# S5 inputs in three PSUM banks instead of two, the turned B and C blocks sharing one region beside y, and scans and y groups one ring step later

## The chip, the core and the metric

The kernel runs on one core of one Trainium2 chip. Its time is device microseconds of one execution, and the number compared is the median of several runs. TensorE (PE) does the matrix products, VectorE (DVE) and ScalarE (ACT) the elementwise work, GpSimd (POOL) some elementwise work on SBUF and the DMA issues of the tables, and SyncE (SP) issues the weight loads. All matmul results go to PSUM, eight banks of 512 float32 columns on each of 128 partitions.

## The reference, cut to what matters

Two transformer-like blocks run one after the other on a sequence of 256 tokens with 2048 features in float32. The change lies in the second one, in its S5 branch, a state space model of 64 groups with 64 complex states each:

```python
bu_re = jnp.einsum('bsgc,gpc->bsgp', uf, bb_re)      # inputs: 16 channels of a group into 64 states
bu_im = jnp.einsum('bsgc,gpc->bsgp', uf, bb_im)
...
_, _, xs_re, xs_im = lax.associative_scan(combine, (a_re, a_im, bu_re, bu_im), axis=1)
y = (jnp.einsum('bsgp,gcp->bsgc', xs_re, c_re.astype(f32))
     - jnp.einsum('bsgp,gcp->bsgc', xs_im, c_im.astype(f32)))
y = y.reshape(bsz, seq, D_SSM) + d_skip.astype(f32) * u.astype(f32)
y = jax.nn.gelu(y.astype(u.dtype))
return y * jax.nn.sigmoid(y @ w_glu + b_glu)
```

The dense products around it (`h @ w_in[l]` above all) fill most of the kernel's time.

## The kernel before, in words

**The ring.** Every dense product streams its weights through a ring of four slots. One ring step (a "subgroup") is two tiles of 128 rows by 512 columns of weights. SP loads it, ACT copies it to `w_hi` (line 658), DVE computes the rest `w_lo = raw - w_hi` (line 1148, `split_lo`), and PE multiplies (lines 1844 to 1847 where the output is by token in 256-column pieces of `h`, lines 1852 to 1854 with 512 columns; 12 matmuls of 512 columns or 24 of 256 a step). ACT and DVE work three steps ahead: in its step s each of them makes the slot of step s+3, and ACT may begin that only when PE is through with step s-1 (`pe_used`). A unit of work is eight steps, and at its end the accumulator is emptied.

**What stands beside the ring.** Other work is hung on ring steps: `places` is a list of (step, function), and in every engine's program the function stands behind that engine's own part of the step. Engines are strictly in order, so this list is the order of work. PE's function for step s stands behind the matmuls of step s, DVE's behind `w_lo` of step s+3. No planner changes it.

**S5.** There are 32 rotations n, each for two groups of states, and they begin at the steps `ROT_AT[n] = 1 + 17*n//8`: 1, 3, 5, 7, 9, 11, 13, 15, 18 and so on, eight rotations in 17 steps. Four rotations with the same n // 4 make a block c of 0 to 7. For one rotation:

- `bu_pair(n)`, for even n, PE at `ROT_AT[n] - 1`: eight small matmuls write the inputs of rotations n and n+1 into the PSUM banks `side[0]` and `side[1]`. It waits for `rot_ready` n, that is until DVE has read the inputs of all rotations up to n-1.
- `rotate_in(n)`, DVE at `ROT_AT[n]`: two multiplies of the bank with a table (lines 1630 and 1631) into one of two buffers, `tmp` or `k_t`.
- POOL adds and subtracts the two products (lines 575 and 576).
- `scan_out(n)`, DVE one step later: two scans (lines 1637 and 1639), and two multiplies into `prods[n % 4]` (line 1643). Behind it POOL issues the load of the table for rotation n+4 (line 567).

For one block c: `turn_b(c)` and `turn_c(c)` transpose the blocks of B and C into PSUM (`tps`), and ACT copies them out (`b_copy`, `c_copy`) three steps ahead of the block's first rotation and three steps behind it. `y_of(c)`, three steps behind the block's last rotation, adds up 16 matmuls into `tps[:, 512:768]`. `skip(c)` on DVE (line 1650), five steps behind the last rotation, reads y out of `tps`, and ACT's `gelu5(c)` follows. The tensor `tps` is two banks, columns 0 to 511 and 512 to 1023. Before the change, B and C lay in the first of them and y in the second.

Of the kernel before, what the change touches and what calls it, by code (L numbers as in the profile page):

```python
# [16 lines left out]
P = 128  # L17
# [4 lines left out]
ACT = mybir.ActivationFunctionType  # L22
# [72 lines left out]
def griffin_block_then_ssm_block(nc, a, inv_freq, out):  # L95
    with ExitStack() as ctx:
        def sb(name, shape, dt=F32):
            return ctx.enter_context(nc.sbuf_tensor(name, shape, dt))
# [7 lines left out]
        def ps(name, shape):  # L106
            return ctx.enter_context(nc.psum_tensor(name, shape, F32))
# [22 lines left out]
        ident = sb("ident", [P, P])  # L130
# [6 lines left out]
        v_tok = sb("v_tok", [P, TT, SEQ])  # L137
# [152 lines left out]
        u_feat, zs = slab_e[:, 0:8, :], slab_e[:, 8:16, :]  # L290
# [12 lines left out]
        c_t = mask[:, :].rearrange("p (n c) -> p n c", n=3)  # L303
        b_t = pi2[:, 0:4, :].rearrange("p a f -> p (a f)").rearrange("p (n c) -> p n c", n=2)
# [320 lines left out]
        ROT_AT = [1 + 17 * n // 8 for n in range(32)]  # L625
# [20 lines left out]
        def _(act):  # L646
# [34 lines left out]
            for rows, tile in ((FIRST_ROWS, 0), (SECOND_ROWS, 1)):  # L681
                at = 0
# [71 lines left out]
            for t in range(TT):  # L754
                ins = nc.scalar.activation(v_tok[:, t, :], tok(acc[0])[:, t, SEQ:2 * SEQ], ACT.Copy, scale=rstd[:, t:t + 1])
# [132 lines left out]
            for c in range(NH):  # L888
# [3 lines left out]
                for t in range(TT):  # L892
                    ins = nc.scalar.activation((tmp, tmp2)[c % 2][:, t, :], tok(acc[u % 2])[:, t, :], ACT.Square,
                                               accum_out=ssq[:, t, c:c + 1])
# [74 lines left out]
            for t in range(TT):  # L969
                act.wait_ge(e_final, t + 1)  # L970
                ins = nc.scalar.activation(tmp[:, t, :], e_tok[:, t, 3 * NC:], ACT.Square, accum_out=ssq[:, t, 3:4])
# [23 lines left out]

            def b_copy(c):
                act.wait_ge(b_turned, c + 1)
                nc.scalar.activation(b_t, tps[:, 0:2 * P].rearrange("p (n c) -> p n c", n=2), ACT.Copy).then_inc(b_copied, 1)

            def c_copy(c):  # L1000
                act.wait_ge(c_turned, c + 1)
                nc.scalar.activation(c_t[:, 0, :], tps[:, 2 * P:3 * P], ACT.Copy)
                nc.scalar.activation(c_t[:, 1:3, :], tps[:, 2 * P:4 * P].rearrange("p (n c) -> p n c", n=2), ACT.Copy,
                                     scale=-1.0).then_inc(c_copied, 1)

            def gelu5(c):
# [8 lines left out]
            places = [(S * (c + 1) + 3, lambda c=c: z_tanh_(c)) for c in range(2)]  # L1015
            for c in range(8):
                at = ROT_AT[4 * c]
# [6 lines left out]
            for c in range(8):  # L1024
# [19 lines left out]
            for c in range(2):  # L1044
# [53 lines left out]
            places = [(1, lambda: qk_copy(0))]  # L1098
# [7 lines left out]
            for i in range(NH):  # L1106
# [3 lines left out]
                for t in range(TT):  # L1110
                    ins = nc.scalar.activation(tmp[:, t, :], tok(acc[U_A % 2])[:, t, :], ACT.Tanh, scale=half_rstd[:, t:t + 1])
# [30 lines left out]
        def _(dve):  # L1142
# [159 lines left out]
            for t in range(TT):  # L1302
                both = stg[:, t, :].rearrange("p (h e u f) -> p h e u f", e=2, u=2, f=32)
                ins = rotate(tok(acc[0]), 4, t, [both[:, :, e] for e in range(2)], t == TT - 1)
# [194 lines left out]
            for c in range(NH):  # L1499
                u = U_OUT + c  # L1500
                at = slice(c * NC, (c + 1) * NC)
# [121 lines left out]
            def rotate_in(n):  # L1623


                t1, t2 = rot[n % 2]
                bu = side[n % 2][:, :].rearrange("p (n c) -> p n c", n=2)
                dve.wait_ge(table_landed[n % 4], 16 * (n // 4 + 1))
                dve.wait_ge(bu_ready, n // 2 + 1)
                V.tensor_tensor(t1, bu, tables[n % 4][:, 0:1, :].broadcast_to([P, 2, SEQ]), ALU.mult)  # L1630
                V.tensor_tensor(t2, bu, tables[n % 4][:, 1:2, :].broadcast_to([P, 2, SEQ]), ALU.mult).then_inc(rot_ready, 1)

            def scan_out(n):
                t1, t2 = rot[n % 2]
                decay = s5p[:, 3, n:n + 1].broadcast_to([P, SEQ])
                dve.wait_ge(mixed_ready, 2 * n + 1)
                chain.mark(V.tensor_tensor_scan(t1[:, 0, :], decay, t1[:, 0, :], 0.0, ALU.mult, ALU.add))  # L1637
                dve.wait_ge(mixed_ready, 2 * n + 2)
                chain.link(V.tensor_tensor_scan(t1[:, 1, :], decay, t1[:, 1, :], 0.0, ALU.mult, ALU.add))
                if n >= 4:  # L1640
                    dve.wait_ge(y5_ready, n // 4)
                for part in range(2):
                    ins = V.tensor_tensor(prods[n % 4][:, 2 * part:2 * part + 2, :], t1,
                                          tables[n % 4][:, part:part + 1, :].broadcast_to([P, 2, SEQ]), ALU.mult)
                ins.then_inc(out_ready, 1)
# [11 lines left out]
            places = [(S * (c - 1) + 1, lambda c=c: u_out(c)) for c in range(2)]  # L1657
            places += [(S * (c + 1) + 2, lambda c=c: z_out(c)) for c in range(2)]
            places += [(S * (c + 1) + 4, lambda c=c: z_silu(c)) for c in range(2)]
            for n in range(32):  # L1660
                places += [(ROT_AT[n], lambda n=n: rotate_in(n)), (ROT_AT[n] + 1, lambda n=n: scan_out(n))]
            for c in range(8):
                at = ROT_AT[4 * c + 3]
                places += [(at + 5, lambda c=c: skip(c)), (at + 7, lambda c=c: gelu_low(c))]
# [27 lines left out]
            for c in range(2):  # L1692
                steps(None, 0, G_GLU + c * 4, {1: [lambda: qk_mean_square(0)]} if c == 0 else {1: [lambda: qk_norm(0)]}, subgroups=4)
                at = slice(c * QPC, (c + 1) * QPC)
# [73 lines left out]
            places = []  # L1768
# [40 lines left out]
            for c in range(NH):  # L1809
# [3 lines left out]
                at = slice(c * NC, (c + 1) * NC)  # L1813
# [7 lines left out]
        def _(pe):  # L1821
            T = nc.tensor
# [198 lines left out]

            def turn_b(c):
                pe.wait_ge(b_ready, c + 1)
                for n in range(2):
                    ins = T.transpose(tps[:, n * P:(n + 1) * P], v_tok[:, 0, n * P:(n + 1) * P], ident[:, :])
                ins.then_inc(b_turned, 1)

            def turn_c(c):
                pe.wait_ge(c_ready, c + 1)
                for n in range(2):  # L2030
                    ins = T.transpose(tps[:, (2 + n) * P:(3 + n) * P], v_tok[:, 1, n * P:(n + 1) * P], ident[:, :])
                ins.then_inc(c_turned, 1)

            def bu_pair(n):

                if n == 0:
                    pe.wait_ge(row_copied, 2)
                if n % 4 == 0:
                    pe.wait_ge(b_copied, n // 4 + 1)
                if n >= 2:  # L2040
                    pe.wait_ge(rot_ready, n)
                for part in range(2):
                    for j in (n % 4, n % 4 + 1):
                        at = slice(32 * j, 32 * j + 32)
                        ins = T.matmul(side[j % 2][:, part * SEQ:(part + 1) * SEQ], b_t[at, part, :], u_feat[at, n // 4, :],
                                       start=True, stop=True)
                ins.then_inc(bu_ready, 1)

            def y_of(c):

                pe.wait_ge(c_copied, c + 1)
                pe.wait_ge(out_ready, 4 * c + 4)
                for n, (c_, q_) in enumerate(((0, 0), (1, 3), (2, 1), (2, 2))):
                    for j in range(4):
                        ins = T.matmul(tps[32 * j:32 * j + 32, NC:NC + SEQ], c_t[:, c_, 32 * j:32 * j + 32], prods[j][:, q_, :],
                                       start=n == 0, stop=n == 3)
                ins.then_inc(y5_ready, 1)

            places = []
            for c in range(8):  # L2060
                at = ROT_AT[4 * c]
                places += [(at - 3, lambda c=c: turn_b(c)), (at + 3, lambda c=c: turn_c(c)),
                           (ROT_AT[4 * c + 3] + 3, lambda c=c: y_of(c))]
            for n in range(0, 32, 2):
                places.append((ROT_AT[n] - 1, lambda n=n: bu_pair(n)))
            beside_s5 = [{2 * s + 1: hooks for s, hooks in of_unit.items()} for of_unit in by_unit(places)]
# [62 lines left out]
            places = [(0, 0, lambda: turn_qk(0))]  # L2129
# [55 lines left out]
```

## Time and profile before

| | us |
|---|---|
| median of 3 runs | 2326.09 (2323.57 to 2327.39) |
| the profiled execution's own time | 2325.59 |
| its span, first to last instruction | 2323.9 |
| PE busy in the span | 2260.1 (97%) |
| DVE busy | 1441.3 (62%) |
| ACT busy | 1196.7 (51%) |
| POOL busy | 400.8 (17%) |

The profile is one execution, and its time lies 0.5 us below the median. An engine that is busy 97% of the span sets the time nearly everywhere. The S5 part lies between 1646 and 1892 us of the span. A row of the timeline gives the start and the length of an instruction, and in brackets the idle time of its engine before it and what ended that. Lengths overlap a little where an engine pipelines, so the pitch from one start to the next is the better price where an engine is busy.

### The profile page before, as it was taken

The page shows a single profiled execution, that of the slowest core. Times are in us where ns is not written, and L with a number is a line of the kernel's source. Part 1 is how long each engine was busy: PE and PEld are TensorE (multiplying, and loading weights), DVE is VectorE, ACT ScalarE, POOL GpSimd, SP SyncE. Part 2 cuts the span into 40 slices and gives each one's busy share as a digit, 9 for nine tenths or more (in the row PEclk, how much of TensorE's full clock was granted, in tenths as well). Part 3 has the DMA queues.
Part 4 walks back from the last instruction along what each step waited for, and adds up shares of the span by engine and source line. Part 5 has one row for each costly group of instructions (what it writes and reads, how often), then busy time and mean ns, then how long its engine had stood idle before and what let it go on. Part 6 is the DMA issues. An engine that isn't in the chain of part 4 may idle for free.

```text
span 2323.9 us, 33022 instructions
## 1 busy us (share of the span) xinstructions
PE 2260.1 (97%) x11754; PEld 1900.5 (82%) x11754; DVE 1441.3 (62%) x1625; ACT 1196.7 (51%) x1851; POOL 400.8 (17%) x408
## 2 busy tenths in 40 slices
PE   7999998999999999999999999998999999999999
PEld 6888988788888778888888888888977778888887
DVE  6666677654554465555555555566799977775554
ACT  5555555644444446555555555555444445554442
POOL 3111484000000102112121121211233321110000
PEclk9999999999999999999999999999999999999999
DMA  8554434566666856666666666665656655556655
GB/s 245 167 150 146 145 120 133 173 190 193 190 191 192 263 164 190 199 204 204 194 209 201 195 205 204 195 207 160 182 171 188 183 173 169 169 163 182 190 188 163
DMA packets 215027, 427.01 MB, mean 184 GB/s; under 512 B 14032, under 2 KB 14320, under 8 KB 214384
## 3 DMA queue, kind: packets, MB, share of 16 engines
q1 hardware_dynamic: 206720, 398.51, 56.1%
q0 software_dynamic: 7744, 26.62, 3.6%
q8 instruction: 83, 1.36, 0.2%
q14 instruction: 48, 0.39, 0.0%
q10 hardware_dynamic: 432, 0.13, 0.0%
HBM read 414.71 MB, written 10.49 MB: 183 GB/s over the span
## 4 chain that ended last, share of the span: by engine, by line
PE 81%; DVE 10%; ACT 3%; issue 2%; POOL 1%; DMA 1%; ACTq 0%; DVEq 0%; POOLq 0%; SPq 0%
PE acc L1852 23%; PE acc L1854 22%; PE acc L1853 22%; DVE w_lo L1148 3%; PE acc L1844 3%; PE acc L1846 3%; PE acc L1847 3%; PE tps L1867 1%; ACT w_hi L658 1%; DMA raw<-in_w_out_dram 1%; POOL k_t L575 1%; POOL tmp L575 1%; PE sides L1923 1%; PE tps L1941 1%; DVE k_t L1637 0%
## 5 line engine op out<-in xcount | busy, mean ns | idle before, releaser
L1148 DVE TENSOR_TENSOR w_lo<-raw,w_hi 128x1024 fp32r<-128x1024 f32 x752 | 947.4, 1264 | 762.5 <-ACT w_hi L658 758.2
L658 ACT ACTIVATE w_hi<-raw 128x1024 fp32r<-128x1024 f32 x752 | 793.9, 1059 | 896.8 <-PE acc L1854 746.8
L1852 PE MATMUL acc<-w_hi,h_hi 128*128 128x512 f32 x1440 | 574.0, 399 | 4.8 <-DVE w_lo L1148 4.2
L1854 PE MATMUL acc<-w_hi,h_lo 128*128 128x512 f32 x1440 | 563.0, 391 | 0.0
L1853 PE MATMUL acc<-w_lo,h_hi 128*128 128x512 f32 x1440 | 562.8, 391 | 0.0
L1852 PEld LDWEIGHTS acc<-w_hi,h_hi 128*128 128x128 f32 x1440 | 271.7, 189 | 73.1 <-issue 12.4
L1854 PEld LDWEIGHTS acc<-w_hi,h_lo 128*128 128x128 f32 x1440 | 271.5, 189 | 58.1
L1853 PEld LDWEIGHTS acc<-w_lo,h_hi 128*128 128x128 f32 x1440 | 272.0, 189 | 53.3
L1852 PE MATMUL acc<-w_hi,slab_dg_r 128*128 128x512 f32 x768 | 300.1, 391 | 3.8 <-DVE w_lo L1148 3.8
L1854 PE MATMUL acc<-w_hi,slab_dg_r 128*128 128x512 f32 x768 | 299.5, 390 | 0.0
L1853 PE MATMUL acc<-w_lo,slab_dg_r 128*128 128x512 f32 x768 | 299.4, 390 | 0.0
L1844 PE MATMUL acc<-h_hi,w_hi 128*128 128x256 f32 x768 | 225.0, 293 | 12.1 <-DVE w_lo L1148 11.9
L1846 PE MATMUL acc<-h_lo,w_hi 128*128 128x256 f32 x768 | 219.9, 286 | 0.0
L1847 PE MATMUL acc<-h_hi,w_lo 128*128 128x256 f32 x768 | 219.7, 286 | 0.0
L1852 PEld LDWEIGHTS acc<-w_hi,slab_dg_r 128*128 128x128 f32 x768 | 144.5, 188 | 34.1 <-issue 4.2
L1854 PEld LDWEIGHTS acc<-w_hi,slab_dg_r 128*128 128x128 f32 x768 | 144.5, 188 | 30.1
L1853 PEld LDWEIGHTS acc<-w_lo,slab_dg_r 128*128 128x128 f32 x768 | 144.6, 188 | 29.9
L1844 PEld LDWEIGHTS acc<-h_hi,w_hi 128*128 128x128 f32 x768 | 149.9, 195 | 19.7 <-DVE w_lo L1148 13.6
L1846 PEld LDWEIGHTS acc<-h_lo,w_hi 128*128 128x128 f32 x768 | 150.1, 195 | 0.2
L1847 PEld LDWEIGHTS acc<-h_hi,w_lo 128*128 128x128 f32 x768 | 149.7, 195 | 0.0
L1852 PE MATMUL acc<-w_hi,slab_f_r 128*128 128x512 f32 x256 | 100.4, 392 | 0.0
L1854 PE MATMUL acc<-w_hi,slab_h_r 128*128 128x512 f32 x256 | 99.7, 389 | 0.0
(371 smaller groups left out, 2335.8 us busy)
## 6 DMA issues: line engine op xcount, KB each, us to landing
raw<-in_w_in_dram SPq DMA_DIRECT2D x328, 512.0 KB, 4.0
raw<-in_w_mlp_up_dram SPq DMA_DIRECT2D x128, 512.0 KB, 3.8
raw<-in_w_mlp_down_dram SPq DMA_DIRECT2D x128, 512.0 KB, 4.7
raw<-in_w_out_dram SPq DMA_DIRECT2D x64, 512.0 KB, 4.3
raw<-in_w_rnn_proj_dram SPq DMA_DIRECT2D x32, 512.0 KB, 4.1
raw<-in_w_attn_proj_dram SPq DMA_DIRECT2D x32, 512.0 KB, 4.7
trig_scratch<-tmp POOLq DMA_DIRECT2D x32, 256.0 KB, 4.0
raw<-in_w_proj_ssm_dram SPq DMA_DIRECT2D x16, 512.0 KB, 3.9
```

Of the source, the lines that this page charges most:

```text
L575: pool.tensor_tensor(t1[:, 0, :], t1[:, 0, :], t2[:, 1, :], ALU.add).then_inc(mixed_ready, 1)
L658: nc.scalar.activation(w_hi[:, j % RING], raw[:, j % RING], ACT.Copy).then_inc(hi_ready, 1)
L1148: V.tensor_tensor(w_lo[:, j % RING], raw[:, j % RING], w_hi[:, j % RING].bitcast(F32), ALU.subtract)\
L1844: T.matmul(o, wh[:, c], hi[:, k, :], start=first and m % 2 == 0, stop=False, skip_group_check=True)
L1846: T.matmul(o, wh[:, c], lo[:, k, :], start=False, stop=False, skip_group_check=True)
L1847: ins = T.matmul(o, wl[:, c], hi[:, k, :], start=False, stop=last, skip_group_check=True)
L1852: T.matmul(o, hi[:, k, c], wh, start=first, stop=False)
L1853: T.matmul(o, hi[:, k, c], wl, start=False, stop=False)
L1854: ins = T.matmul(o, lo[:, k, c], wh, start=False, stop=last)
L1867: ins = T.transpose(tps[:, b * SEQ + t * P:b * SEQ + (t + 1) * P], stg[:, t, b * P:(b + 1) * P], ident[:, :])
L1923: ins = T.matmul(side[n][:, t * P:t * P + (t + 1) * P], q_c[at, p, t * P:(t + 1) * P], k_c[at, 0:(t + 1) * P], start=True, stop=True)
L1941: ins = T.matmul(y_banks[64 * n:64 * n + 64, t, :], v_c[:, s, :], prob_t[p % 2][:, n, b * P:(b + 1) * P], start=s == 0, stop=s == t)
```

## The change

- The inputs of the rotations go in turn into three banks, `side[0]`, `side[1]` and the first bank of `tps`. `bu_pair(n)` therefore waits for `rot_ready` n-1 instead of n.
- The turned B and the turned C use one region, `tps[:, 768:1024]`, one after the other. It lies in the bank of y. Waits keep them apart: `turn_b(c)` waits until C of block c-1 is copied, `turn_c(c)` until B of block c is copied and until y of block c-1 is read (`y5_read`), and `y_of(c)` until B of block c+1 is copied.
- `scan_out(n)` stands two steps behind `ROT_AT[n]` instead of one, and `y_of(c)` four steps behind the block's last rotation instead of three. `skip`, `turn_b`, `turn_c`, `bu_pair` and `rotate_in` keep their steps.

```diff
+        bu_banks, bc_bank = [side[0], side[1], tps[:, 0:NC]], tps[:, NC + SEQ:]
...
-                bu = side[n % 2][:, :].rearrange("p (n c) -> p n c", n=2)
+                bu = bu_banks[n % 3][:, :].rearrange("p (n c) -> p n c", n=2)
...
-                places += [(ROT_AT[n], lambda n=n: rotate_in(n)), (ROT_AT[n] + 1, lambda n=n: scan_out(n))]
+                places += [(ROT_AT[n], lambda n=n: rotate_in(n)), (ROT_AT[n] + 2, lambda n=n: scan_out(n))]
...
             def turn_b(c):
                 pe.wait_ge(b_ready, c + 1)
+                if c:
+                    pe.wait_ge(c_copied, c)
...
             def turn_c(c):
                 pe.wait_ge(c_ready, c + 1)
+                pe.wait_ge(b_copied, c + 1)
+                if c:
+                    pe.wait_ge(y5_read, c)
...
                 if n >= 2:
-                    pe.wait_ge(rot_ready, n)
+                    pe.wait_ge(rot_ready, n - 1)
...
-                        ins = T.matmul(side[j % 2][:, part * SEQ:(part + 1) * SEQ], b_t[at, part, :], u_feat[at, n // 4, :],
+                        bank = bu_banks[(n + j % 2) % 3]
+                        ins = T.matmul(bank[:, part * SEQ:(part + 1) * SEQ], b_t[at, part, :], u_feat[at, n // 4, :],
...
                 pe.wait_ge(c_copied, c + 1)
+                if c < 7:
+                    pe.wait_ge(b_copied, c + 2)
                 pe.wait_ge(out_ready, 4 * c + 4)
...
-                           (ROT_AT[4 * c + 3] + 3, lambda c=c: y_of(c))]
+                           (ROT_AT[4 * c + 3] + 4, lambda c=c: y_of(c))]
```

In DVE's program before, around `skip(2)` (line 1650); `k_t<-sides` is rotation 13 coming in, the two SCALAR_TENSOR_TENSOR rows are its scans, and the names in brackets are the semaphores waited for:

```order
L1148 TENSOR_TENSOR w_lo<-raw,w_hi 128x1024 [waits hi_ready]
L1630 TENSOR_TENSOR k_t<-sides,stg 128x512 [waits bu_ready,table_landed1]
L1631 TENSOR_TENSOR k_t<-sides,stg 128x512
L1148 TENSOR_TENSOR w_lo<-raw,w_hi 128x1024 [waits hi_ready]
L1637 SCALAR_TENSOR_TENSOR k_t<-s5p,k_t 128x256 [waits mixed_ready]
L1639 SCALAR_TENSOR_TENSOR k_t<-s5p,k_t 128x256 [waits mixed_ready]
L1643 TENSOR_TENSOR slab_f_f<-k_t,stg 128x512 [waits y5_ready,v_chain]
L1643 TENSOR_TENSOR slab_f_f<-k_t,stg 128x512
L1650 SCALAR_TENSOR_TENSOR k_c<-slab_e_f,pt,tps 128x256 [waits y5_ready]
L1148 TENSOR_TENSOR w_lo<-raw,w_hi 128x1024 [waits hi_ready]
```

The same place of the changed program (its lines stand one higher):

```order
L1631 TENSOR_TENSOR k_t<-sides,stg 128x512 [waits bu_ready,table_landed1]
L1632 TENSOR_TENSOR k_t<-sides,stg 128x512
L1149 TENSOR_TENSOR w_lo<-raw,w_hi 128x1024 [waits hi_ready]
L1651 SCALAR_TENSOR_TENSOR k_c<-slab_e_f,pt,tps 128x256 [waits y5_ready]
L1149 TENSOR_TENSOR w_lo<-raw,w_hi 128x1024 [waits hi_ready]
L1638 SCALAR_TENSOR_TENSOR k_t<-s5p,k_t 128x256 [waits mixed_ready]
L1640 SCALAR_TENSOR_TENSOR k_t<-s5p,k_t 128x256 [waits mixed_ready]
L1644 TENSOR_TENSOR slab_f_f<-k_t,stg 128x512 [waits y5_ready,v_chain]
L1644 TENSOR_TENSOR slab_f_f<-k_t,stg 128x512
L1631 TENSOR_TENSOR tmp<-tps,tmp 128x512 [waits bu_ready,table_landed2]
```

Two `w_lo` now stand between a rotation and its scans, the scans are followed at once by the next rotation, and `skip(2)` stands ahead of the scans of rotation 13 instead of behind them.

In PE's program before, at the transposes `turn_c(3)` (line 2031), with the last matmul of the ring step before them and the first of the next:

```order
L1854 MATMUL acc<-w_hi,h_lo 128x512
L2031 MATMUL tps<-ident,v_tok 128x128 [waits c_ready]
L2031 MATMUL tps<-ident,v_tok 128x128
L2045 MATMUL sides<-slab_e_f,pi 128x256 [waits rot_ready]
L2045 MATMUL sides<-slab_e_f,pi 128x256 x3
L1852 MATMUL acc<-w_hi,h_hi 128x512 [waits lo_ready]
```

And in the changed program:

```order
L1855 MATMUL acc<-w_hi,h_lo 128x512
L2037 MATMUL tps<-ident,v_tok 128x128 [waits y5_read,b_copied,c_ready]
L2037 MATMUL tps<-ident,v_tok 128x128
L2052 MATMUL tps<-slab_e_f,pi 128x256 [waits rot_ready]
L2052 MATMUL sides<-slab_e_f,pi 128x256
L2052 MATMUL tps<-slab_e_f,pi 128x256
L2052 MATMUL sides<-slab_e_f,pi 128x256
L1853 MATMUL acc<-w_hi,h_hi 128x512 [waits lo_ready]
```

Nothing has moved here except that `turn_c(3)` now also waits for `y5_read`, which `skip(2)` gives, and stands in front of the inputs of rotations 14 and 15 and of the whole next ring step.

## Rows read from the trace of the kernel before

**Rows 1.** Windows: busy us of PE, PEld, DVE, ACT, POOL; granted clock; DMA

```profile
1768.00:1828.00 60.00, 56.91 (x303) 43.55 (x302) 55.97 (x70) 26.71 (x47) 22.51 (x24) 0.97 0.61 184
1649.50:1890.00 240.50, 229.05 (x1364) 184.17 (x1363) 224.42 (x277) 108.94 (x182) 91.46 (x92) 0.99 0.59 177
```

**Rows 2.** Waits from 1618 to 1905 us: total us, times, longest us

```profile
PE sides L2045 <- DVE k_t L1631: 7.9, 5, 2.3
...
DVE k_t L1637 <- POOL k_t L575: 6.8, 11, 0.6
...
DVE tmp L1637 <- POOL tmp L575: 6.3, 10, 0.6
```

**Rows 3.** Timeline of DVE, one rotation's length of work

```profile
1799.17 1.29 DVE L1643 TENSOR_TENSOR slab_dg_f<-k_t,tmp 128x512 f32<-128x512 f32 x2
1800.39 1.22 DVE L1148 TENSOR_TENSOR w_lo<-raw,w_hi 128x1024 fp32r<-128x1024 f32 x1
1801.52 0.68 DVE L1630 TENSOR_TENSOR tmp<-sides,stg 128x512 f32<-128x512 f32 x1
...
1802.72 1.22 DVE L1148 TENSOR_TENSOR w_lo<-raw,w_hi 128x1024 fp32r<-128x1024 f32 x1
1804.56 1.21 DVE L1637 TENSOR_TENSOR_SCAN tmp<-s5p,tmp 128x256 f32<-128x256 f32 x1 [0.62 <-POOL tmp L575]
1805.69 0.66 DVE L1639 TENSOR_TENSOR_SCAN tmp<-s5p,tmp 128x256 f32<-128x256 f32 x1
```

**Rows 4.** Timeline of POOL at the same place

```profile
1802.90 1.63 POOL L575 TENSOR_TENSOR tmp<-tmp 128x256 f32<-128x256 f32 x1 [1.57 <-DVE tmp L1631]
1804.48 0.73 POOL L576 TENSOR_TENSOR tmp<-tmp 128x256 f32<-128x256 f32 x1
```

**Rows 5.** Timeline of DVE and POOL, two DVE operations before the scan; a scan without POOL

```profile
1687.99 1.75 DVE L1621 SCALAR_TENSOR_TENSOR slab_e_f<-slab_dg_f 128x1024 f32<-128x1024 f32 x1
1689.66 1.22 DVE L1637 TENSOR_TENSOR_SCAN k_t<-s5p,k_t 128x256 f32<-128x256 f32 x1
...
1820.21 0.68 DVE L1637 TENSOR_TENSOR_SCAN tmp<-s5p,tmp 128x256 f32<-128x256 f32 x1
...
1688.62 1.72 POOL L576 TENSOR_TENSOR k_t<-k_t 128x256 f32<-128x256 f32 x1
```

**Rows 6.** Timeline of PE and of DVE at block 3

```profile
1750.03 0.38 PE L2031 MATMUL tps<-ident,v_tok 128*128 128x128 f32 x2
1750.34 1.13 PE L2045 MATMUL sides<-slab_e_f,pi 32*128 32x256 f32 x8
...
1754.90 0.47 DVE L1650 SCALAR_TENSOR_TENSOR k_c<-slab_e_f,pt,tps 128x256 f32<-128x256 f32 x1
```

**Rows 7.** Timeline of PE, six matmuls apart; a copy of ACT at a unit's end

```profile
1726.97 0.39 PE L1854 MATMUL acc<-w_hi,h_lo 128*128 128x512 f32 x1
...
1728.33 0.39 PE L1854 MATMUL acc<-w_hi,h_lo 128*128 128x512 f32 x1
...
1729.44 1.27 ACT L1033 ACTIVATE slab_dg_f<-acc,small 128x512 f32<-128x512 f32 x2 [1.60 <-PE acc L1854]
1730.60 1.06 ACT L658 ACTIVATE w_hi<-raw 128x1024 fp32r<-128x1024 f32 x1
```

**Rows 8.** Timeline of PE behind three long waits

```profile
384.38 0.58 PE L1844 MATMUL acc<-h_hi,w_hi 128*128 128x256 f32 x1 [2.96 <-DVE w_lo L1148]
...
1721.04 1.40 PE L2045 MATMUL sides<-slab_e_f,pi 32*128 32x256 f32 x8 [2.32 <-DVE k_t L1631]
...
1890.42 0.41 PE L2055 MATMUL tps<-slab_f_f,mask 128*32 128x256 f32 x2 [2.37 <-DVE slab_dg_f L1643]
```

**Rows 9.** Windows behind the first two of these waits, columns as in rows 1

```profile
390.00:392.00 2.00, 2.00 (x17) 2.00 (x16) 0.27 (x1) 1.99 (x5) 0.00 (x0) 0.86 0.51 116
...
1721.00:1722.00 1.00, 0.96 (x8) 0.68 (x8) 1.00 (x2) 0.56 (x2) 0.92 (x2) 0.89 0.87 338
...
1725.00:1726.00 1.00, 1.00 (x5) 0.77 (x5) 1.00 (x3) 0.00 (x0) 0.00 (x0) 0.91 0.98 379
```

More of the change, by code:

```diff
@@ L997, in b_copy @@
                 act.wait_ge(b_turned, c + 1)
-                nc.scalar.activation(b_t, tps[:, 0:2 * P].rearrange("p (n c) -> p n c", n=2), ACT.Copy).then_inc(b_copied, 1)
+                nc.scalar.activation(b_t, bc_bank.rearrange("p (n c) -> p n c", n=2), ACT.Copy).then_inc(b_copied, 1)
             def c_copy(c):
                 act.wait_ge(c_turned, c + 1)
-                nc.scalar.activation(c_t[:, 0, :], tps[:, 2 * P:3 * P], ACT.Copy)
-                nc.scalar.activation(c_t[:, 1:3, :], tps[:, 2 * P:4 * P].rearrange("p (n c) -> p n c", n=2), ACT.Copy,
+                nc.scalar.activation(c_t[:, 0, :], bc_bank[:, 0:P], ACT.Copy)
+                nc.scalar.activation(c_t[:, 1:3, :], bc_bank.rearrange("p (n c) -> p n c", n=2), ACT.Copy,
                                      scale=-1.0).then_inc(c_copied, 1)
@@ L2023, in turn_b @@
                 pe.wait_ge(b_ready, c + 1)
+                if c:
+                    pe.wait_ge(c_copied, c)
                 for n in range(2):
-                    ins = T.transpose(tps[:, n * P:(n + 1) * P], v_tok[:, 0, n * P:(n + 1) * P], ident[:, :])
+                    ins = T.transpose(bc_bank[:, n * P:(n + 1) * P], v_tok[:, 0, n * P:(n + 1) * P], ident[:, :])
                 ins.then_inc(b_turned, 1)
@@ L2029, in turn_c @@
                 pe.wait_ge(c_ready, c + 1)
+                pe.wait_ge(b_copied, c + 1)
+                if c:
+                    pe.wait_ge(y5_read, c)
                 for n in range(2):
-                    ins = T.transpose(tps[:, (2 + n) * P:(3 + n) * P], v_tok[:, 1, n * P:(n + 1) * P], ident[:, :])
+                    ins = T.transpose(bc_bank[:, n * P:(n + 1) * P], v_tok[:, 1, n * P:(n + 1) * P], ident[:, :])
                 ins.then_inc(c_turned, 1)
```

## The prediction

> **What bounds the kernel now.** The page says PE, 97% busy. The change touches only the S5 part, so I read that part alone, in windows: over its 240.5 us PE is busy 229.05 and DVE 224.42 [rows 1]. PE has 11.45 us without work there, so PE is not the only bound. The reader is to see in the waits whom PE waits for: DVE, 7.9 us in 5 waits of `bu_pair` for `rot_ready` [rows 2]. That is the wait that the third bank removes. DVE waits in turn for POOL, 6.8 + 6.3 us in 21 waits ahead of a scan [rows 2], which the later scans remove. Is DVE the bound? I add up its program for 8 rotations (17 steps) from the pitches of its timeline [rows 3]: two multiplies 1.22, `w_lo` 1.13, the rotation 1.20, `w_lo` with the wait 1.84, the scans 1.13 and about 0.68 make 7.20 a rotation. Eight are 57.6; a seventeenth `w_lo` adds 1.1, `skip` twice 0.9 [rows 6], and `gelu_low` (line 1655, 256 columns, so half of a 512-column 0.68) twice 0.7: 60.3. The window of such a length, 1768 to 1828, is 60.0, with DVE's record at 55.97 and PE's at 56.91 [rows 1]; the missing 4 us of DVE are its waits for POOL and one for ACT. So DVE's chain, with what POOL takes out of it, sets the pace in S5, and PE has 3.1 us to spare in 60. The clock of 0.97 in that window says that 0.03 x 60 = 1.8 us of PE's 56.9 are matmuls at a lowered clock, so PE needs about 55.1 at the full one.
>
> **The change, part by part.** The sum is made against the profiled execution's 2325.59 us; the median of before is 0.5 higher.
>
> *No more wait of `bu_pair`.* It frees PE, not DVE. Since DVE is the chain, PE only comes sooner to its next wait for DVE. I take 0. If DVE were not the chain it would be worth up to the 7.9 us.
>
> *Scans one step later, on DVE.* Now a rotation goes through `w_lo`, a wait of 0.62, and a scan of 1.21 [rows 3], while alone a scan takes 0.68 [rows 5]. POOL's first addition is recorded with 1.63, its second with 0.73 [rows 4]: the first sat behind DVE's `w_lo`, and the second held up the scan. POOL thus costs DVE 1.84 - 1.13 = 0.71, plus 0.53 in the scan, 1.24 together. With two `w_lo` between rotation and scan the trace has a close relative, a `w_lo` and then a two-input operation of the same size ahead of the scan: that operation takes 1.75 instead of about 1.22, the scan 1.22 instead of 0.68, and POOL's second addition 1.72 [rows 5]. POOL then costs 0.53 + 0.54 = 1.07. The stall goes into `w_lo`; only 0.17 is saved, at most at the 21 rotations with a wait: -3.6 us. In the Trainium skill, "SBUF — State Buffer", section "Who interferes with whom", a vector instruction with two SBUF inputs and a GpSimd instruction that reads SBUF exclude each other, and the second blocks fully until the first is over. The rows agree in kind (the first addition took 1.63), and it speaks against this part: moving the scan can't hide the additions. By its word two additions of 0.73 would cost DVE 1.46 a rotation, 0.22 more than the 1.24 of now, and this term would be +4.6; by the rows it is -3.6.
>
> POOL's own queue: its issue of a table load waits for the products, and moves with them by a step. The table is needed three rotations later, some 21 us by the 7.20 above, so the load stays hidden: 0. Were it not, the rotation would wait on DVE, the chain. At the start the ring is not yet full, and the first scan stands behind a `w_lo` that must wait for PE: +0.5, an estimate, since only one step of 2.7 us is involved and POOL's part falls into it.
>
> *`turn_c` waits for `y5_read`.* This is the new wait. Behind it in PE's queue stand the inputs of two rotations and the next step's 12 matmuls; ACT's `c_copy` waits for it, and through `pe_used` all of ACT's and DVE's later slots. Now `turn_c(3)` runs at 1750.03 and `skip(2)` ends at 1755.37 [rows 6], 5.3 us later. In the changed program the skip comes ahead of two scans and two multiplies (about 3.0 us), but PE no longer loses time at `bu_pair` (3.1 us in 60). So PE will stand about as long as all its slack: 60 - 55.1 = 4.9, less what the clock takes, some 3 to 5 us at a stretch. That happens at odd blocks (1, 3, 5, 7), where `y_of` to `turn_c` is one ring step; at even blocks there are two steps, and PE comes about as late as the skip: 0.
>
> Does it reach DVE? Count from the end of the skip. PE: transposes and inputs 1.4 [rows 6], two steps of 2 x 1.36 = 2.72 [rows 7], then ACT's `w_hi` 1.06 [rows 7] and two hand-overs of about 0.1: 8.1 us until DVE may make the slot after next. DVE has in hand: `w_lo` 1.13, the rest of POOL 0.9, scans, multiplies and a rotation 3.7, `w_lo` 1.13, the gelu rest 0.35, POOL 1.07: 8.25 us. So it just fits, and everything that makes PE slower after the stand goes straight into DVE's chain. Two things do. A unit's end puts ACT's two copies, 1.16 [rows 7], in front of `w_hi`: it falls into this stretch whole at block 3 and in part at 1 and 5, +1.7. And the clock.
>
> *The clock after a stand.* After a wait of 2.32 the granted clock fell from 2.4 to 1.2 GHz: of five windows of 1 us the first has 0.89, the last 0.91 and the three between them 0.50, so it was low from about 1721.8 to 1725.2 [rows 8, 9], which costs half of 3.4 us, 1.7. After a wait of 2.96 PE resumed at 384.38 and the clock, at 0.50 all the time, was back only at about 390.6 (0.86 in the window from 390 to 392) [rows 8, 9]: up to 3.1. After 2.37 at 1890.42 it did not fall [rows 8]. Today such a loss is covered by PE's slack. At `turn_c` it isn't. With stands above 3 us I take 2.0 each, nearer the row in the same stage, and 3.5 of the four blocks, since the first stand is short (2.8 by the same count): +7.0. At block 7 it is PE's path to the end of S5 that pays. There the last `y_of` waits for DVE 2.37 us today [rows 8]; with one more ring step in front of it PE should come after DVE, and my count from the last skip gives the same length as now within 0.3: 0, between -2.4 and +2.7 (one step).
>
> Sum: -3.6 + 0.5 + 1.7 + 7.0 = +5.6, or 2331.2 us; I say 2331.0.
>
> **The rivals.**
> 1. *The stand at `turn_c` costs DVE through the clock* (above), chance 0.50. Its own range: three blocks at 1.7 give -1.4 + 5.1 = +3.7, four at 3.1 give +11.0, so 2329 to 2337.
> 2. *The stand is harmless*: the clock holds, as at 1890.42, or rises before the second step, chance 0.30. Then -3.6 + 0.5 + 1.7 = -1.4: 2324.2, with 2322 to 2327 around it.
> 3. *The other side, faster*: POOL's additions find gaps and DVE loses nothing to them. The condition is that `w_lo` waits for ACT when the additions are due, so that they run beside nothing. DVE's chain would shrink by up to 32 x 1.24 = 40 us, PE becomes the bound, and its 11.45 us of idle time [rows 1] vanish: 2314.1. It decides from 0.09 us a rotation on top of rival 2 (2.8 us in 32). Against it stands that DVE has no idle time for 57 of 60 us. Chance 0.10, with all that lies below 2321.4.
> 4. *Each addition holds DVE for its full 0.73*, 1.46 instead of 1.24: the first term turns from -3.6 to 21 x 0.22 = +4.6, and the sum to 2339.4. This is what the SBUF page of the Trainium skill would make of it. The 1.75 and 1.22 of rows 5 speak against it. Chance 0.05.
> 5. *The change does nothing*: PE is late anyhow, the wait for `y5_read` finds it given, and DVE's 0.17 do not show: 2325.6, chance 0.05.
>
> **How the numbers follow.** A measurement of this kernel tells about 0.2%, 4.7 us, from no change, so the bounds are 2321.4 and 2330.7. Rival 1 lies above with two thirds of its chance, 4 wholly; 2, 5 and the rest of 1 lie within: slower 0.40, same 0.50, faster 0.10. The range for 8 in 10 goes from rival 2's low end to rival 1's high end: 2322 to 2337. Cases of both signs hold most of the chance, and the likeliest one's own range is 2329 to 2337.
>
> **What would show it.** The waits of PE for DVE's `rot_ready` at the inputs are gone; in their place a wait at the transposes of C, 3 to 5 us at blocks 3, 5 and 7, released by `skip`, with the granted clock at 0.5 behind it for 3 to 6 us. DVE's waits for POOL ahead of the scan are gone, and the `w_lo` second behind a rotation is recorded with 1.7 instead of 1.22. DVE shows waits for ACT's `w_hi`, 1 to 3 us, two slots behind each odd skip. Eight rotations take 61 to 62 us. I am wrong if DVE's rotations come at under 59 us per eight (rival 3), if PE's long stand is elsewhere, at `y_of` or at the ring's own wait, or if the stands are under 2 us.

## The result and the profile after

| | before | after |
|---|---|---|
| median of 5 runs, us | 2325.78 (2323.57 to 2327.39) | 2335.50 (2335.41 to 2338.12) |
| profiled execution's span, us | 2323.9 | 2333.7 |
| mean granted clock | 0.991 | 0.988 |

The changed kernel is slower: ratio 1.0044 with a 95% interval from 1.0033 to 1.0055, some 10 us. That lies in the range of the prediction, 4.5 us above its central value, and on the side of rival 1.

The windows of the changed kernel. The first two rows answer to [rows 1]; the others are 2 us each around the transposes of C of block 3.

```profile
1649.50:1890.00 240.50, 225.05 (x1318) 178.91 (x1317) 217.41 (x264) 104.70 (x178) 103.78 (x90) 0.96 0.59 171
1768.00:1828.00 60.00, 56.83 (x302) 42.92 (x302) 56.42 (x68) 26.06 (x47) 27.35 (x24) 0.97 0.62 179
...
1754.00:1756.00 2.00, 0.54 (x2) 0.29 (x2) 2.00 (x3) 0.62 (x2) 2.00 (x2) 0.85 0.52 133
1756.00:1758.00 2.00, 2.00 (x9) 1.18 (x8) 2.00 (x3) 0.71 (x3) 1.17 (x1) 0.50 0.85 240
1758.00:1760.00 2.00, 2.00 (x7) 1.55 (x6) 1.97 (x4) 0.00 (x0) 0.07 (x1) 0.50 0.83 214
1760.00:1762.00 2.00, 2.00 (x6) 1.59 (x5) 0.83 (x2) 0.00 (x0) 1.57 (x3) 0.50 0.52 120
1762.00:1764.00 2.00, 2.00 (x10) 1.59 (x9) 0.00 (x0) 0.90 (x1) 0.33 (x1) 0.95 0.20 82
```

In the same 240.5 us both engines do less than before: PE 225.05 for 229.05, DVE 217.41 for 224.42, though PE's sum holds matmuls stretched by a clock of 0.96 (before 0.99). So the time is lost inside S5: from the first rotation to the end of the span the kernel before takes 674.4 us, the changed one 684.4. DVE, which sets the pace of S5, stands more.

The waits of the changed kernel from 1618 to 1905 us, for [rows 2]:

```profile
DVE w_lo L1149 <- ACT w_hi L659: 40.5, 27, 3.9
...
PE tps L2037 <- DVE k_c L1651: 15.4, 6, 4.1
```

The waits for `rot_ready` and for POOL are gone. In their place PE waits 15.4 us at `turn_c` (line 2037) for `skip` (line 1651). The six waits are 4.09, 3.08, 2.85 and 3.78 us at blocks 1, 3, 5 and 7, and 1.33 and 0.31 at blocks 2 and 4. The text calls such a wait of PE a stand. Block 3 in PE's timeline, then in DVE's and ACT's:

```profile
1755.46 0.66 PE L2037 MATMUL tps<-ident,v_tok 128*128 128x128 f32 x2 [3.08 <-DVE k_c L1651]
...
1758.65 0.63 PE L1854 MATMUL acc<-w_lo,h_hi 128*128 128x512 f32 x1
...
1762.84 0.39 PE L1853 MATMUL acc<-w_hi,h_hi 128*128 128x512 f32 x1
```

```profile
1754.85 0.47 DVE L1651 SCALAR_TENSOR_TENSOR k_c<-slab_e_f,pt,tps 128x256 f32<-128x256 f32 x1
1755.24 1.35 DVE L1149 TENSOR_TENSOR w_lo<-raw,w_hi 128x1024 fp32r<-128x1024 f32 x1
1756.51 1.21 DVE L1638 TENSOR_TENSOR_SCAN k_t<-s5p,k_t 128x256 f32<-128x256 f32 x1
...
1760.15 0.68 DVE L1632 TENSOR_TENSOR tmp<-tps,tmp 128x512 f32<-128x512 f32 x1
1764.19 1.23 DVE L1149 TENSOR_TENSOR w_lo<-raw,w_hi 128x1024 fp32r<-128x1024 f32 x1 [3.37 <-ACT w_hi L659]
1765.34 0.42 DVE L1656 TENSOR_TENSOR slab_h_r<-slab_e_f,slab_f_r 128x256 fp32r<-128x256 f32 x1
1768.02 1.23 DVE L1149 TENSOR_TENSOR w_lo<-raw,w_hi 128x1024 fp32r<-128x1024 f32 x1 [2.26 <-ACT w_hi L659]
```

```profile
1763.10 1.06 ACT L659 ACTIVATE w_hi<-raw 128x1024 fp32r<-128x1024 f32 x1 [6.39 <-PE acc L1855]
...
1765.77 1.27 ACT L1034 ACTIVATE slab_dg_f<-acc,small 128x512 f32<-128x512 f32 x2 [0.67 <-PE acc L1855]
1766.93 1.06 ACT L659 ACTIVATE w_hi<-raw 128x1024 fp32r<-128x1024 f32 x1
```

This is the whole chain. PE stands 3.08 us, and its clock is at 0.50 from about 1755.4 to 1762.2 (matmuls of 0.63 instead of 0.39). ACT may make the next slot only when that slow ring step is over, at 1763.10, so DVE stands 3.37 us. ACT's two copies at the unit's end then put the slot after it late: 2.26 more. At block 1 the same two waits are 3.86 and 1.32, at block 5 2.92 and 0.46.

The clock was low for 6.8, 6.8, 3.4 and 3.4 us at blocks 1, 3, 5 and 7. I work that out from the 2-us windows: above, 0.15 + 3 x 0.50 + 0.05 of clock is missing, each worth 2 / 0.5 us, 6.8 together.

One rotation of the changed kernel where no stand is near, for [rows 3] and [rows 4]:

```profile
1801.59 0.69 DVE L1631 TENSOR_TENSOR k_t<-sides,tmp 128x512 f32<-128x512 f32 x1
...
1802.79 2.89 DVE L1149 TENSOR_TENSOR w_lo<-raw,w_hi 128x1024 fp32r<-128x1024 f32 x2
1805.61 1.23 DVE L1638 TENSOR_TENSOR_SCAN k_t<-s5p,k_t 128x256 f32<-128x256 f32 x1
1806.76 0.66 DVE L1640 TENSOR_TENSOR_SCAN k_t<-s5p,k_t 128x256 f32<-128x256 f32 x1
...
1808.66 0.68 DVE L1631 TENSOR_TENSOR tmp<-tps,stg 128x512 f32<-128x512 f32 x1
...
1802.96 1.64 POOL L576 TENSOR_TENSOR k_t<-k_t 128x256 f32<-128x256 f32 x1 [0.43 <-DVE k_t L1632]
1804.57 1.72 POOL L577 TENSOR_TENSOR k_t<-k_t 128x256 f32<-128x256 f32 x1
```

Two `w_lo` take a pitch of 2.82 instead of twice 1.13, and the scan 1.15 instead of about 0.6. A rotation comes 7.07 us after the one before it, where [rows 3] gave 7.20.

### The profile page after: what moved, and what is told of

Read it like the earlier page. It is cut to its first block, busy times and chain, and to the rows that moved or that the text cites. A ratio compares the mean times of both kernels' runs of the same rounds, so it can differ in the third digit from the quotient of the medians.

```text
span 2333.7 us, 33037 instructions
## 1 busy us (share of the span) xinstructions
PE 2265.7 (97%) x11754; PEld 1902.6 (82%) x11754; DVE 1443.4 (62%) x1625; ACT 1197.5 (51%) x1851; POOL 415.2 (18%) x408
## 4 chain that ended last, share of the span: by engine, by line
PE 83%; DVE 9%; ACT 4%; issue 2%; DMA 1%; ACTq 0%; POOL 0%; DVEq 0%; POOLq 0%; SPq 0%
PE acc L1853 23%; PE acc L1855 23%; PE acc L1854 23%; DVE w_lo L1149 3%; PE acc L1845 3%; PE acc L1847 3%; PE acc L1848 3%; ACT w_hi L659 1%; PE tps L1868 1%; DMA raw<-in_w_out_dram 1%; PE sides L1924 1%; PE tps L1942 1%; DVE tmp L1390 0%; PE tps L1935 0%; DVE tmp L1638 0%
## 5 line engine op out<-in xcount | busy, mean ns | idle before, releaser
L1853 PEld LDWEIGHTS acc<-w_hi,h_hi 128*128 128x128 f32 x1440 | 272.1, 189 | 74.1 <-issue 15.3
```

Source lines behind the costliest of these rows:

```text
L1853: T.matmul(o, hi[:, k, c], wh, start=first, stop=False)
```

## The experiments

Each run was compared with the kernel before on the same chip; the last columns are from its profiled execution: the start of DVE's first rotation (its first multiply), that of the last skip, their difference, called the length of S5, and the time from the first rotation to the end of the span. The last skip is not at the same distance from the end in every kernel: 426.2 or 426.3 us where scans and y stand at their old steps, 427.5 to 428.7 where they stand later. Between two kernels of different steps only the last column compares like with like; it also leaves out what differs ahead of S5. It is one execution of each.

| run | median us | ratio to before (95%) | first | last | S5 | first to end |
|---|---|---|---|---|---|---|
| before | | | 1649.52 | 1897.66 | 248.1 | 674.4 |
| after | 2335.50 | 1.0044 (1.0033 to 1.0055) | 1649.32 | 1905.42 | 256.1 | 684.4 |
| e1_turn_c_later | 2324.37 | 0.9991 (0.9982 to 1.0000) | 1648.97 | 1894.27 | 245.3 | 672.8 |
| e2_old_steps | 2351.51 | 1.0099 (1.0084 to 1.0115) | 1652.36 | 1924.50 | 272.1 | 698.4 |
| e3_scans_y_later | 2325.89 | 0.9997 (0.9988 to 1.0006) | 1649.77 | 1896.68 | 246.9 | 674.4 |
| e4_skip_sooner | 2325.47 | 0.9995 (0.9986 to 1.0004) | 1649.16 | 1894.73 | 245.6 | 674.2 |
| e5_wait_alone | 2349.75 | 1.0097 (1.0081 to 1.0112) | 1650.50 | 1922.18 | 271.7 | 697.9 |
| e6_all_later | 2321.45 | 0.9976 (0.9966 to 0.9986) | 1650.29 | 1892.22 | 241.9 | 669.4 |
| e7_inputs_first | 2327.66 | 1.0003 (0.9994 to 1.0012) | 1647.36 | 1895.22 | 247.9 | 676.2 |
| e8_inputs_thrice | 2326.42 | 0.9996 (0.9987 to 1.0005) | 1651.30 | 1896.64 | 245.3 | 673.6 |
| e9_filled | 2329.83 | 1.0007 (0.9998 to 1.0016) | 1647.93 | 1899.18 | 251.3 | 679.6 |
| e10_later_sooner | 2319.98 | 0.9966 (0.9952 to 0.9979) | 1651.41 | 1891.37 | 240.0 | 668.7 |
| e11_banks_later | 2326.63 | 0.9995 (0.9986 to 1.0004) | 1652.10 | 1899.92 | 247.8 | 674.0 |

Theory A was that the stand at `turn_c`, and the low clock behind it, is the whole loss. Rival B was that the later scans and y cost the time, rival C that ACT's copies at a unit's end do.

### The wait with nothing else, and without the later scans

The kernel before with one wait added (e5_wait_alone):

```diff
             def turn_c(c):
                 pe.wait_ge(c_ready, c + 1)
+                if c:
+                    pe.wait_ge(y5_read, c)
```

> The kernel before with one wait added: the transposes of C also wait for y of the block before to be read. Two banks, all steps as before. Theory A: PE stands 3 to 5 us at blocks 1, 3, 5 and 7 and less at even ones, the clock falls behind it, 2333 to 2342. Rival B (the wait is harmless, the later scans or y cost it): 2324 to 2328.

The changed kernel with scans and y at their old steps (e2_old_steps):

```diff
-                places += [(ROT_AT[n], lambda n=n: rotate_in(n)), (ROT_AT[n] + 2, lambda n=n: scan_out(n))]
+                places += [(ROT_AT[n], lambda n=n: rotate_in(n)), (ROT_AT[n] + 1, lambda n=n: scan_out(n))]
...
-                           (ROT_AT[4 * c + 3] + 4, lambda c=c: y_of(c))]
+                           (ROT_AT[4 * c + 3] + 3, lambda c=c: y_of(c))]
```

> The changed kernel with scans and y at their old steps: only the three banks, the shared region and its waits are left. The skip stands at the same ring step, so the wait for y read is as late as before. Theory A: stands of 3 to 5 us at blocks 1, 3, 5 and 7, time 2332 to 2339 (about 3 us more than the changed kernel if the scans' shift saved the forecast 3.6). Rival B (the later scans and y cost it): 2323 to 2327, as before.

Both are 24 us longer than before, in S5 and to the end, so the wait alone does it, and the third bank takes none of it away. Rival B falls: without the later scans the wait costs more than twice what it costs with them (10.0 us to the end), more than I had expected. The stands are longer, 5.30 to 5.75 us at the odd blocks of the wait alone, and so is the low clock behind them: 10.2, 10.2, 6.8 and 6.8 us, 34 together, half of which is 17 of the 24. PE's and DVE's timelines of the wait alone at block 3:

```profile
1762.14 0.66 PE L2033 MATMUL tps<-ident,v_tok 128*128 128x128 f32 x2 [5.35 <-DVE k_c L1650]
...
1761.52 0.48 DVE L1650 SCALAR_TENSOR_TENSOR k_c<-slab_e_f,pt,tps 128x256 f32<-128x256 f32 x1
1761.91 1.22 DVE L1148 TENSOR_TENSOR w_lo<-raw,w_hi 128x1024 fp32r<-128x1024 f32 x1
1764.93 0.69 DVE L1630 TENSOR_TENSOR tmp<-sides,tmp 128x512 f32<-128x512 f32 x1 [1.80 <-PE sides L2047]
...
1771.42 1.23 DVE L1148 TENSOR_TENSOR w_lo<-raw,w_hi 128x1024 fp32r<-128x1024 f32 x1 [5.21 <-ACT w_hi L658]
```

Here the skip stands behind the scans. When it frees PE, DVE has one `w_lo` left in hand and stands 1.80 us for the inputs and 5.21 for ACT. In the changed kernel the scans stand behind the skip and cover part of PE's way.

### Taking the stand away

The transposes of C later at the odd blocks (e1_turn_c_later), then at all blocks (e6_all_later):

```diff
-                places += [(at - 3, lambda c=c: turn_b(c)), (at + 3, lambda c=c: turn_c(c)),
+                places += [(at - 3, lambda c=c: turn_b(c)), (at + 3 + 2 * (c % 2), lambda c=c: turn_c(c)),   # e1
+                places += [(at - 3, lambda c=c: turn_b(c)), (at + 4 + c % 2, lambda c=c: turn_c(c)),         # e6
```

(`c_copy` moves by as many steps; the two added lines are those of two kernels, marked with their names here.)

> The changed kernel with the transposes of C and their copy two ring steps later at the odd blocks (1, 3, 5, 7). The wait for y read then lies some 5.4 us later than the skip needs. Theory A (the stand at the transposes of C, and the low clock behind it, is the whole loss): stands of 3 to 4 us gone, clock 0.99 in S5, DVE's waits for w_hi of over 2 us gone, time 2320 to 2326, at or below the kernel before. Rival B (the later scans and y cost it, through POOL or a longer end of S5): stays at 2333 to 2336 even with the stands gone. Rival C (ACT's two copies at a unit's end in front of w_hi are the larger part): 2330 to 2333, with DVE's waits for w_hi still above 2 us at blocks 1, 3 and 5.

> The changed kernel with the transposes of C and their copy one ring step later at even blocks and two at odd ones (the run with odd blocks alone had three stands left, 4.4, 1.9 and 0.9 us, all at even blocks). Theory A: no stand left over 1 us, clock 1.00 throughout S5, 2319 to 2324, a little below the run with the odd blocks alone. If PE's slack then just goes into one wait elsewhere (at y or at the ring) and the clock falls there: 2323 to 2327.

e1 is 11 us shorter in S5 than the changed kernel. Of its stands three are left, all at even blocks; the first is 4.39 us, since PE now comes there sooner. e6 has 0.4 us left of them, and eight rotations take 58.6 us from `skip(2)` to `skip(4)`. Its windows:

```profile
1708.00:1768.00 60.00, 57.29 (x310) 43.07 (x309) 59.34 (x71) 27.56 (x49) 28.29 (x24) 1.00 0.60 179
1768.00:1828.00 60.00, 58.52 (x316) 44.36 (x315) 59.32 (x72) 27.39 (x48) 28.76 (x25) 1.00 0.63 191
```

DVE is busy 59.3 of 60 us and the clock is 1.00. Short waits of PE elsewhere are left, 3.1 us at `turn_b` for ACT's copy and 4.2 at `y_of`, and the clock does not fall behind them. Theory A holds: the stand gone, the same change is 0.24% faster than before. Rival C falls as a cause by itself, for the copies are still there.

DVE's skip one ring step sooner (e4_skip_sooner), and the same on top of e6 (e10_later_sooner):

```diff
-                places += [(at + 5, lambda c=c: skip(c)), (at + 7, lambda c=c: gelu_low(c))]
+                places += [(at + 4, lambda c=c: skip(c)), (at + 7, lambda c=c: gelu_low(c))]
```

> The changed kernel with DVE's skip one ring step sooner (four steps behind the last rotation, the step of y). y is ready before the stand begins, so DVE frees the region about 3 us sooner. Theory A: stands under 1 us, the clock stays at 1.00, 2321 to 2327. Rival B: 2333 to 2336. A third outcome: DVE now waits for PE's y at the skip, up to 1 us at 8 blocks, which puts the time at 2328 to 2332.

> The run with all transposes of C later (0.9976 of the kernel before) and also the skip one ring step sooner. In the run with the sooner skip alone DVE waited for PE's y at three blocks, 2.5 us in all. If those waits lie on DVE's chain: 2323 to 2326, slower than without. If the last stand at the transposes (0.4 us at block 2) and the end of S5 matter more: 2318 to 2321.

e4 is as good as e1, but not as I had expected: PE still stands at the four odd blocks, 1.30, 3.75, 2.18 and 2.41 us. e10 has the skip at the same place and no stands, so it prices those of e4: from `skip(0)` to `skip(2)`, `skip(2)` to `skip(4)` and `skip(4)` to `skip(6)` e4 takes 61.9, 61.7 and 59.1 us, e10 62.0, 58.6 and 58.6. At blocks 1 and 5 the clock of e4 held, and the stands cost 0 and 0.5 us: the skip that ends them now comes a ring step sooner in DVE's program, with a `w_lo` more behind it. At block 3 it was low for 6.8 us, and 3.1 are lost. What a stand costs is set by what DVE has in hand when it ends, and by the clock behind it. e10 is the best of all, 0.34% below before. DVE no longer waits for y, because PE is early there; it is PE that waits at `y_of` (line 2064), up to 1.8 us. A new wait shows beside it in its waits:

```profile
ACT w_hi L659 <- DMA raw<-in_w_in_dram: 22.2, 10, 3.9
...
PE tps L2064 <- DVE slab_dg_f L1644: 7.1, 4, 1.8
```

ACT waits for the weights' loads, 22.2 us in 10 waits (e6: 5.2 in 2), so S5 is now near the next limit.

### The clock apart from the stand

Inputs ahead of the transposes (e7_inputs_first), and the same with the inputs' matmuls three times over at odd blocks (e8_inputs_thrice):

```diff
-            places = []
+            places = [(ROT_AT[n] - 1, lambda n=n: bu_pair(n)) for n in range(0, 32, 2)]
...
-            for n in range(0, 32, 2):
-                places.append((ROT_AT[n] - 1, lambda n=n: bu_pair(n)))
...
-                for part in range(2):
+                for part in [0, 1] * (3 if n % 8 == 6 else 1):                          # e8 only
```

> The changed kernel with the inputs of the next two rotations ahead of the transposes of C where both stand at one ring step. The stand stays, shorter by 1.1 us, and PE has 1.1 us less to do behind it. Theory A: four odd blocks give back about 1.1 us each, 2330 to 2333, with the granted clock still at 0.5 behind the stands.

> As the run with the inputs ahead of the transposes, but at the odd blocks the eight matmuls of the inputs are done three times over, which writes the same values again and fills 2.1 us of the stand with work. If the lowered clock behind the stand is a large part of the loss (1.5 to 3 us at each odd block by the granted clock of the changed kernel's trace, 9 us together): the clock stays nearer 1.00 there and the time falls below the run without the filling by 3 to 8 us, to 2323 to 2328. If the stand itself is the loss, the same time or up to 2 us more than without the filling.

e7 gives back 8.2 us of S5, not 4.4, because the clock's low stretch is now 3.4 us at each of the four stands; block 3 in its windows:

```profile
1749.00:1751.00 2.00, 0.40 (x3) 0.43 (x3) 2.00 (x3) 0.48 (x2) 1.98 (x2) 0.82 0.54 131
1751.00:1753.00 2.00, 2.00 (x7) 1.62 (x6) 2.00 (x3) 0.85 (x3) 1.32 (x1) 0.50 0.85 239
1753.00:1755.00 2.00, 2.00 (x8) 1.59 (x8) 1.97 (x4) 0.00 (x0) 0.00 (x0) 0.83 0.77 219
```

In e8 the clock stayed at 1.00 at blocks 5 and 7 and fell at 1 and 3, for 3.4 us each. S5 is 2.5 us shorter than in e7; the ratios (0.9996 and 1.0003) don't tell the two apart. So I changed only the clock, with the changed kernel's order kept (e9_filled): 24 matmuls, whose results the real inputs write again, ahead of `turn_c` at odd blocks. The last two lines of the edit are cut to the part that differs.

```diff
+            def fill(n):
+                pe.wait_ge(rot_ready, n - 1)
+                for part in [0, 1] * 3:
+                    for j in (n % 4, n % 4 + 1):
+                        at = slice(32 * j, 32 * j + 32)
+                        T.matmul(bu_banks[(n + j % 2) % 3][:, part * SEQ:(part + 1) * SEQ], b_t[at, part, :],
+                                 u_feat[at, n // 4, :], start=True, stop=True)
...
-(at + 3, lambda c=c: turn_c(c))
+(at + 3, lambda c=c: (fill(4 * c + 2) if c % 2 else None, turn_c(c)))
```

> The changed kernel, all in its order, with 24 matmuls (three times the eight of the next inputs, 3.2 us) ahead of the transposes of C at the odd blocks, so that they fill the stand; the real inputs still follow behind. In the changed kernel the clock was low for about 6.9, 7.3, 3.0 and 3.1 us behind the four stands, 20 us together, which halves the work done in them. If the clock is the loss: it stays at 1.00 at most of the four places and the time comes to 2323 to 2329. If it is the stand by itself (PE's work and ACT's copies held up until y is read): 2333 to 2337.

The filling held the clock at blocks 3 and 5, not at 1 and 7, and the time, 2329.8, lies between my two forecasts. Its timelines at block 1 (the first row) and block 3, and then a window behind each:

```profile
1689.35 0.66 PE L2037 MATMUL tps<-ident,v_tok 128*128 128x128 f32 x2 [1.31 <-DVE k_c L1651]
...
1753.91 0.41 PE L2037 MATMUL tps<-ident,v_tok 128*128 128x128 f32 x2 [0.26 <-DVE k_c L1651]
...
1759.54 1.65 DVE L1149 TENSOR_TENSOR w_lo<-raw,w_hi 128x1024 fp32r<-128x1024 f32 x1 [0.26 <-ACT w_hi L659]
1761.11 0.96 DVE L1656 TENSOR_TENSOR slab_h_r<-slab_e_f,slab_f_r 128x256 fp32r<-128x256 f32 x1
1763.36 1.22 DVE L1149 TENSOR_TENSOR w_lo<-raw,w_hi 128x1024 fp32r<-128x1024 f32 x1 [1.28 <-ACT w_hi L659]
```

```profile
1690.00:1692.00 2.00, 2.00 (x10) 1.18 (x9) 1.97 (x4) 0.60 (x3) 0.00 (x0) 0.50 0.31 72
...
1754.00:1756.00 2.00, 2.00 (x13) 1.36 (x14) 2.00 (x2) 1.07 (x4) 1.62 (x1) 1.00 0.58 161
```

That makes a comparison inside one run, from the starts of `skip`:

| | before | after | e9_filled | e6 | clock low in after, in e9 |
|---|---|---|---|---|---|
| `skip(0)` to `skip(2)`, with block 1 | 62.2 | 64.7 | 64.6 | 60.3 | 6.8, 6.8 |
| `skip(2)` to `skip(4)`, with block 3 | 60.0 | 63.2 | 60.1 | 58.6 | 6.8, 0 |
| `skip(4)` to `skip(6)`, with block 5 | 60.1 | 62.1 | 60.5 | 59.7 | 3.4, 0 |

Where the clock held, 3.1 and 1.6 us came back. That is nearly half of 6.8 and of 3.4, all that a half-speed clock can cost PE, and it reaches DVE. Where it fell, next to nothing came back. What stays above e6 (1.5 and 0.8) is what the stand costs at the full clock, ACT's copies at the unit's end included.

### What carries the gain

The kernel before with scans and y later, two banks (e3_scans_y_later), and e6 with scans and y at their old steps (e11_banks_later). The edits are those of the change and of e2.

> The kernel before with only its scans and y groups one ring step later; two banks, B and C in their own bank, no new waits. What the forecast's first term says (POOL costs a rotation 1.07 instead of 1.24 us): 2321 to 2326. If the third bank is what makes the shift possible: PE waits at the inputs for rot_ready as before, 8 us in all, hidden. If the later y costs at the end of S5: 2327 to 2330. No stand at the transposes of C in any case.

> The run with all transposes of C later, but scans and y at their old steps: three banks and shared region alone, with the new wait out of the way. If the later scans carry the gain (POOL's 1.24 against 1.07 at each rotation): 2325 to 2329, as before or just above, with DVE's waits for POOL at the scan back. If the third bank alone carries it: 2319 to 2323. A stand of 1 us or more may stay at the transposes, since the skip stands behind two scans there: then up to 2335.

Neither part alone gives anything that can be measured; both together (e6) give 0.24%. On top of the later scans the third bank, with the transposes moved out of the way, is worth 5.0 us to the end (674.4 to 669.4), with the old steps next to nothing (674.4 to 674.0). In e3 PE's wait for `rot_ready` has grown from 7.9 to 10.6 us, up to 3.1 at a time, and the clock is at 0.97 in three of four windows of about 60 us, before in two. That this is what eats the gain there is likely, not shown. In e11 DVE waits for POOL as before (7.5 + 6.3). e11 is not quite free of new waits: PE waits 5.7 us at `turn_b` for ACT's copy, up to 2.3 at a time, and the clock was low for 3.4 us once; DVE's waits for `w_hi` are 24.0 us, before 25.5. The waits of e3, then of e11:

```profile
PE sides L2045 <- DVE k_t L1631: 10.6, 6, 3.1
```

```profile
DVE k_t L1638 <- POOL k_t L576: 7.5, 12, 0.6
DVE tmp L1638 <- POOL tmp L576: 6.3, 10, 0.6
```

## Why the prediction was right, and where it was off

- **No more wait of `bu_pair`: 0.** Right with the old steps: e11 has the bank without the stand and gains nothing. Together with the later scans it is not 0: there it makes the difference between e3 and e6, 5.0 us. The forecast priced the two parts one by one.
- **Scans later, -3.6, and the start, +0.5.** The mechanism was right: POOL costs DVE 0.56 in the two `w_lo` and about 0.55 in the scan, 1.11 where 1.07 was forecast. So the stall went into `w_lo` and was not hidden. In the Trainium skill, "SBUF — State Buffer", section "Who interferes with whom", a blocked instruction waits for the whole of the other; two additions of 0.73 would then cost 1.46, by an estimate, and the rows don't bear that out. The term was too small: e6, where nothing long stands in its way, is 5.0 us shorter to the end than before, against 3.1. The 0.13 between 7.20 and 7.07 holds at all 32 rotations instead of 0.17 at 21, 4.2 us; the other 0.8 I can't place.
- **Stands of 3 to 5 us at odd blocks, little at even ones.** Right in place, releaser and size (2.9 to 4.1), except that the first is the longest, not the shortest.
- **Does it reach DVE: 8.25 us in hand against PE's 8.1, and ACT's copies +1.7.** The terms in hand add up to 8.28. At the full clock the count nearly held. In e9 at block 3, from the end of `skip(2)` at 1753.76 to the second awaited `w_lo` at 1763.36, 9.6 us pass, where the forecast has 8.1 and 1.16 for the copies. DVE works 8.1 of them and stands 0.26 + 1.28. In its 8.1 is 0.97 of POOL's additions, seen in a `w_lo` of 1.57 and a gelu rest of 0.97 instead of 0.42. In the changed kernel the same additions (POOL, from 1760.92, 0.73 and 0.72) run while DVE stands for ACT: they cover nothing, and its work from 1755.32 to 1768.02 is 1.19 + 4.24 + 1.15 + 0.42 = 7.0 of 12.7. That is 3.1 more than the 9.6 of e9, nearly half of the 6.8 of low clock. Against e6 the stands cost at the full clock 1.5 us at block 3, 0.8 at block 5 and, by an estimate, 0.9 at block 1 (64.6 less 60.3, less half of 6.8): 3.2, where the forecast had 1.7. No run takes the copies away, so their own share stays an estimate.
- **The clock, 3.5 blocks x 2.0 = 7.0.** This is the term that was most mis-sized; it was right in kind. Four blocks, low for 6.8, 6.8, 3.4 and 3.4 us, half of it 10.2. [Rows 9] held both lengths, and I took the shorter for nearly all.
- **The end of S5, 0.** Too small as well. From `skip(6)` to the end of the span the changed kernel takes 453.6 us, e6 450.1. Of the 3.5 between them the low clock behind block 7 can be 1.7, so 1.8 is the stand's own.

In the profiled executions, from the first rotation to the end, the changed kernel is 10.0 us longer than before; the forecast was 5.6. The clock (+3.2), the stands at the full clock (+1.5) and the end (+1.8), less the larger gain (-1.9), come to +4.6, where 4.4 are missing. The mechanism was right, but that the time lies inside the range owes something to luck: with the gain that was forecast it would have been some 2337.4 us, just outside.

Rival 2, the harmless stand, falls: e6 is 15.0 us shorter than the changed kernel without the stand, and e9 shows 3.1 and 1.6 of it to be the clock alone. Rivals 3 and 4 fall by the rotation's 7.07: it would be 7.20 - 1.24 = 5.96 with the additions hidden, and 7.42 with 1.46. Rival 5 falls by the interval, 1.0033 to 1.0055. The forecast gave "slower by more than 0.2%" a chance of 0.40 and no change beyond it 0.50; the second leant on rival 2.

## What to carry to other kernels

A wait added on an in-order engine is safe if what gives it comes before the engine gets there. Where the engine comes first, look at what the engine that sets the pace has in hand, and move the waiting work, not the data: one or two ring steps turned 0.44% slower into 0.24% faster. Count the clock in: the four stands of 2.9 to 4.1 us were followed by 3.4 to 6.8 us at half clock, and with no slack nearly half of that is lost on top. Stalls that come from a third engine are no safe part of what a starved engine has in hand: they stayed in e9, where it stood 0.26 us ahead of them, and were gone in the changed kernel, where it stood 3.37. Two parts of a change that each give nothing can give something together, so undo them one at a time from the best version, not only from the first.

## What the hardware showed that I had not expected

- The low clock behind stands had more than one length. In the changed kernel it lasted 6.8 us behind blocks 1 and 3, with PE busy all the while, and 3.4 behind 5 and 7; in e5, behind longer stands of 5.75 and 5.35 us, 10.2. With the inputs moved ahead (e7), it was 3.4 at all four, which made a move of 1.1 us worth 2.1 at each block.
- Twenty-four small matmuls (32 rows) in place of a stand kept the clock at two blocks. At block 1 of e9 it fell all the same, behind a wait of 1.31, and stayed at 0.50 for 6.8 us. In e8 it fell behind waits of 1.36 and 1.28 and held behind one of 1.51. Why it falls in one case and not in the other is open.
